# Two layers written out one after the other: the last output products moved behind the barrier into the next layer's block, weights loaded across it, the copy of x dropped

## The chip, the cores and the metric

The kernel runs on one core of one Trainium2 chip. The metric is the device time of one execution in microseconds (us), the median of several runs. The core has a matrix engine (TensorE, PE in the rows), a vector engine (VectorE, DVE), a scalar engine (ScalarE, ACT), GpSimd (POOL) and a sync engine (SyncE, SP) that issues DMA. Each engine works through its own list of instructions in order. They meet only at semaphores: an instruction can wait until a counter has reached a value, and raises a counter when it is done.

## The reference

The input x is 512 tokens of 2048 float32 features. Two layers are applied. `h` is the RMS norm of x; one projection makes everything else; four mixers (RWKV-7, mLSTM, latent attention, differential attention) produce 512 features each, gated by `silu(z)`:

```python
h = RMSNorm(x);  p = h @ W_in            # 2048 x about 7900
# p -> [ z | RWKV-7 group | mLSTM group | MLA group | differential-attention group ]
y = concat(beta_A*A, beta_B*B, beta_C*C, beta_D*D) * silu(z)
x = x + y @ W_out                        # 2048 x 2048
```

Layer 0 and layer 1 differ in one place of the RWKV-7 group. Layer 0 keeps its `v` as `v_first`. Layer 1 mixes it in:

```python
if v_res is None:
    v_first = v
else:
    v0, v_dn, v_up = v_res
    v = v + (v_first - v) * jax.nn.sigmoid(v0 + (v @ v_dn) @ v_up)
```

## The kernel before

All large products are made in three parts, since each float32 operand is split into a high and a low half (`w_hi`, `w_lo` for weights, `h_hi`, `h_lo` for activations). A weight step is one block of 128 rows by up to 512 columns. SP loads it into one of six `raw` buffers, the high half is made by ACT (`high_part`, L1234) in the first 32 steps and the last ones of a layer and by POOL (L746) in between, and POOL makes the low half (L756) into one of four split buffers. A step has four tiles (column blocks, or token blocks for the output), and a tile is three matmuls of 128x512. A layer has 256 steps of the projection (`project`, L785), and 64 of the output: 48 early ones (`out_early`), for the first twelve blocks of y, and 16 of the tail, for the last four (all `out_product`, L800). A group of 16 projection steps fills a PSUM bank per tile; ACT copies it out (`evacuate`, L1225) and stores it to DRAM, from where the mixers load it.

The mixers run in between on the same engines. Their small products depend on DVE and ACT, and PE fills the waits with projection tiles. The order is written out by hand: the table `FILL` says how many tiles PE takes at each named place of each head (`fill(name, h)`), and `planned` deals them out. Places named `to_...` take whatever is missing to the end of a group, so that a number changed ahead of one is paid back there. The last place is `rest`, which takes the remaining early output tiles.

The program starts with a block of its own. SP loads x (four tiles `x_tok`), parameters and constants, and copies x to the output in DRAM. ACT squares x (L424). Then comes a loop `nc.Fori(0, DEPTH)`, whose body is executed twice. In it: the mean of the squares (DVE L1601), its inverse root by `rstd` (ACT L1269, L1270, Ln and Exp, each with a table load), the diagonal (DVE L1614), a product with ones that spreads it (PE L837), a copy (ACT L1277), and the transposes of x (PE L834, L843) scaled by DVE (`scale_h`, L1621). Near the end of the layer x is loaded again from the output. `add_tile` (DVE L1893) adds finished output tiles to it. The tail, the last lines of the PE block, follows `rest`; `keep_x` on ACT stores x and squares it (L1547). Then all engines meet at a barrier that also clears the layer's semaphores (POOL L1953), and the loop jumps back.

Heads of RWKV-7 are taken in pairs `hp` of 0 to 3. PE waits there at L942 (for the gate of the pair before, DVE L1594), at L948 (for DVE L1709) and at L952 (for DVE L1740). `tanh_z` (ACT L1256) must run before the gate. At L917 the scores of the latent attention wait for DVE L1665, at L1156 those of the differential attention for ACT L1500.

In this kernel layer 0 mixes v as well, with a factor of zero (`half_flag`), since both layers are the same code.

Of the kernel before, what the change touches and what calls it, by code (L numbers as in the profile page):

```python
# [27 lines left out]
P = 128  # L28
# [45 lines left out]
TAIL = 4 * (len(OUT_PARTS) - 1)  # L74
EARLY = sum(q < TAIL for q, *_ in OUT)
# [4 lines left out]

Y_LOADS = STEPS - KT + 3 + N_RAW + N_SPLIT


def tiles_of(g):
    return 3 if g == G_MISC else 4


PROJ_TILES = [(n, m) for n in range(STEPS) for m in range(tiles_of(n // KT))]
# [10 lines left out]
    da_first=17, da_sums=(16, 10, 10, 10), da_scores=(8, 6, 6, 6), da_half=(13, 15, 18, 18), da_turned=(3, 3, 3, 3),  # L99
# [211 lines left out]
def build(nc, a, out):  # L311

    with ExitStack() as ctx:
# [81 lines left out]
        half_flag = small[:, 60:61]  # L395
        lam_init = small[:, 61:62]
        one_m_lam_init = small[:, 62:63]

        s_setup, s_setup_out, s_flags = sem("setup_loaded"), sem("x_kept"), sem("flags_set")
        s_setup_squared = sem("setup_squared")
        s_params_loaded = sem("params_loaded")
        s_setup_x = [sem(f"x_loaded_{i}") for i in range(NT)]
        neg_f32 = carve(D, P)

        with nc.Block() as block:
            @block.sync
            def _(sp):  # L410
                for i in range(NT):
                    sp.dma_start(x_tok[:, i, :], a["x"][0, i * P:(i + 1) * P, :]).then_inc(s_setup_x[i], 16)
                sp.dma_start(par_all[:], a["params"]).then_inc(s_params_loaded, 16)
                sp.dma_start(always[:], a["const"][:, 0:ALWAYS]).then_inc(s_setup, 16)
                sp.dma_start(neg_f32, a["const"][:, CONST["neg"][0]:CONST["neg"][0] + P]).then_inc(s_setup, 16)

                sp.dma_start(out[0], a["x"][0]).then_inc(s_setup_out, 16)

            @block.scalar
            def _(act):  # L420
                act.wait_ge(s_flags, 1)
                for i in range(NT):
                    act.wait_ge(s_setup_x[i], 16)
                    nc.scalar.activation(carve(0, D), x_tok[:, i, :], ACT.Square, accum_out=ms_parts[:, i, 0:1]  # L424
                                         ).then_inc(s_setup_squared, 1)
                    act.wait_ge(s_setup_squared, i + 1)

            @block.vector
            def _(dve):
                nc.vector.memset(small[:, 64:80], 0.0).then_inc(s_flags, 1)  # L430
                nc.vector.memset(v_first[:], 0.0).then_inc(s_flags, 1)
                nc.vector.memset(small[:, 0:60], 0.0).then_inc(s_flags, 1)
                nc.vector.memset(half_flag, 0.0).then_inc(s_flags, 1)
                nc.vector.memset(lam_init, 0.8 - 0.6).then_inc(s_flags, 1)
                nc.vector.memset(one_m_lam_init, 1.0 - (0.8 - 0.6)).then_inc(s_flags, 1)
                dve.wait_ge(s_setup, 32)
                nc.vector.tensor_copy(mask_ident, ident).then_inc(s_flags, 1)
                nc.vector.tensor_copy(neg, neg_f32).then_inc(s_flags, 1)
                dve.wait_ge(s_flags, 8)


# [81 lines left out]
        x_junk = da_pt[:, 0, :]  # L523
# [25 lines left out]

        s_lam_ready = sem("lam_ready")  # L550
        s_h_hi_ready = sem("h_hi_ready")
        s_par_ready = sem("par_ready")
        s_x_squares = sem("x_squares")
# [8 lines left out]
        s_hi_split = sem("hi_split")  # L562
        s_hi_by_act = sem("hi_by_act")
# [3 lines left out]
        s_raw_split = sem("raw_split")  # L567
        s_split_used = sem("split_used")
# [4 lines left out]
        s_out_kept = sem("out_kept")  # L573
# [115 lines left out]
        s_raw_loaded = [sem(f"raw_loaded_{s}") for s in range(N_RAW)]  # L689
# [12 lines left out]
        weight_steps = list(steps_of_weights())  # L702
# [7 lines left out]
        with nc.Fori(0, DEPTH) as layer:  # L710
            with nc.Block() as block:
                @block.sync
                def _(sp):

                    for n, (source, k, pieces) in enumerate(weight_steps):
                        part, early = divmod(n - Y_LOADS, 3)
                        if 0 <= part < 4 and early == 0:
                            ks = slice(3 * part, 3 * part + 3)
                            sp.wait_ge(s_split_used, STEPS - KT + 3 * part + 3)
# [6 lines left out]
                        if n >= N_RAW:  # L726
                            sp.wait_ge(s_raw_split, n - N_RAW + 1)
                        at = 0
                        for c0, width in pieces:
                            sp.dma_start(raw[:, n % N_RAW, at:at + width],  # L730
                                         a[source][layer, k * P:(k + 1) * P, c0:c0 + width]
                                         ).then_inc(s_raw_loaded[n % N_RAW], 16)
                            at += width

                @block.gpsimd
                def _(pool):

                    for n in range(len(weight_steps)):
                        pool.wait_ge(s_raw_loaded[n % N_RAW], raw_target[n])
                        if n >= N_SPLIT:  # L740
                            pool.wait_ge(s_split_used, n - N_SPLIT + 1)
# [18 lines left out]
                def _(pe):  # L760
# [52 lines left out]
                    def out_early(n, i):  # L813
                        q, c, k, first, _ = OUT[n - STEPS]
                        if i == 0:
                            pe.wait_ge(s_raw_split, n + 1)
                            if c == 0:
                                wait_y(k)
# [372 lines left out]
                    for n in range(STEPS + EARLY, ALL_STEPS):  # L1191
                        q, c, k, first, _ = OUT[n - STEPS]
                        if c == 0:
                            wait_y(k)
# [782 lines left out]
```

## Time and profile before

| | |
|---|---|
| median of 3 runs | 2497.51 us (2495.53 to 2502.27) |
| the profiled execution | 2498.22 us |
| its span, first to last instruction | 2496.5 us |
| mean granted TensorE clock | 0.982 of full speed |
| PE busy | 96% of the span |
| DVE, ACT, POOL busy | 47%, 25%, 69% |
| HBM traffic | 116 GB/s over the span |

A row of the timeline gives start, duration, engine, line, operation, operands and in brackets how long the engine was idle before it and what ended that wait. The projected end of a matmul is modelled, so that successive ones overlap in the rows.

### The profile page before, as it was taken

How to read it: one execution, taken by the hardware profiler on the slowest of the kernel's cores; microseconds unless marked ns; L12 is line 12 of the kernel's file. 1: busy time of each engine (PE TensorE's matmuls, PEld its weight loads, DVE VectorE, ACT ScalarE, POOL GpSimd, SP SyncE). 2: the span in 40 equal slices, each digit the busy share in tenths (PEclk: the TensorE clock that was granted, in tenths of full speed). 3: DMA queues.
4: the chain of work that ended last, by engine and by line, in shares of the span. 5: the costliest groups of instructions: out<-in, count | busy, mean ns of one | idle time of the engine just before them, and what ended most of it. 6: DMA issues, size and time to landing. Idle time of an engine off the chain costs nothing. (4 is left out here: it accounts for less than half of the span.)

```text
span 2496.5 us, 40525 instructions
## 1 busy us (share of the span) xinstructions
PE 2390.7 (96%) x16332; PEld 1798.2 (72%) x16332; DVE 1183.6 (47%) x1654; ACT 632.1 (25%) x1119; POOL 1724.5 (69%) x1228
## 2 busy tenths in 40 slices
PE   6999999999999999999979999999999999999998
PEld 4766677676777777777867677777777767777777
DVE  5122236656473774454260232376465637735442
ACT  4222212212121222333242223112121112223423
POOL 2675588567585877877636666877575767877875
PEclk9999999999999999999989999999999999999999
DMA  6622344223233435632336232532232234465323
GB/s 213 181 80 74 95 141 123 73 86 89 82 106 106 132 114 180 213 85 72 118 96 185 80 102 77 166 94 82 73 106 83 85 115 131 127 213 163 85 76 122
DMA packets 164293, 288.69 MB, mean 116 GB/s; under 512 B 29017, under 2 KB 36569, under 8 KB 162497
## 3 DMA queue, kind: packets, MB, share of 16 engines
q1 hardware_dynamic: 108864, 185.51, 26.5%
q10 hardware_dynamic: 55232, 100.51, 11.7%
q8 instruction: 130, 2.13, 0.4%
q14 instruction: 67, 0.54, 0.1%
HBM read 234.29 MB, written 55.84 MB: 116 GB/s over the span
## 5 line engine op out<-in xcount | busy, mean ns | idle before, releaser
L746 POOL TENSOR_SCALAR w_hi<-raw 128x512 fp32r<-128x512 f32 x552 | 897.2, 1625 | 547.7 <-PE ps_proj L785 481.5
L756 POOL TENSOR_TENSOR w_lo<-raw,w_hi 128x512 fp32r<-128x512 f32 (+1 forms) x640 | 831.9, 1301 | 174.0 <-ACT w_hi L1234 127.9
L785 PE MATMUL ps_proj<-h_hi,w_hi 128*128 128x512 f32 (+1 forms) x1760 | 735.6, 418 | 20.2 <-POOL w_lo L756 9.9
L785 PE MATMUL ps_proj<-h_lo,w_hi 128*128 128x512 f32 (+1 forms) x1760 | 691.6, 393 | 0.0
L785 PE MATMUL ps_proj<-h_hi,w_lo 128*128 128x512 f32 x1728 | 679.6, 393 | 0.0
L785 PEld LDWEIGHTS ps_proj<-h_hi,w_hi 128*128 128x128 f32 (+1 forms) x1760 | 332.0, 189 | 125.8 <-issue 38.2
L785 PEld LDWEIGHTS ps_proj<-h_lo,w_hi 128*128 128x128 f32 (+1 forms) x1760 | 332.6, 189 | 74.0 <-issue 11.6
L785 PEld LDWEIGHTS ps_proj<-h_hi,w_lo 128*128 128x128 f32 x1728 | 327.3, 189 | 71.8
L800 PE MATMUL ps_proj<-w_hi,h_hi 128*128 128x512 f32 x448 | 183.1, 409 | 3.9 <-DVE arena L1893 3.9
L800 PE MATMUL ps_proj<-w_hi,h_lo 128*128 128x512 f32 x448 | 175.3, 391 | 0.0
L800 PE MATMUL ps_proj<-w_lo,h_hi 128*128 128x512 f32 x448 | 174.7, 390 | 0.0
L1225 ACT ACTIVATE stage<-ps_proj 128x512 f32<-128x512 f32 (+1 forms) x118 | 70.5, 597 | 252.9 <-PE ps_proj L785 200.4
L785 PE MATMUL ps_proj<-w_hi,h_hi 128*128 128x512 f32 x256 | 107.6, 420 | 0.4 <-ACT stage L1225 0.4
L785 PE MATMUL ps_proj<-w_lo,h_hi 128*128 128x512 f32 x256 | 101.7, 397 | 0.0
L800 PEld LDWEIGHTS ps_proj<-w_hi,h_hi 128*128 128x128 f32 x448 | 84.3, 188 | 24.2 <-issue 8.1
L785 PE MATMUL ps_proj<-w_hi,h_lo 128*128 128x512 f32 x256 | 101.4, 396 | 0.0
L800 PEld LDWEIGHTS ps_proj<-w_lo,h_hi 128*128 128x128 f32 x448 | 84.4, 188 | 19.7 <-issue 3.4
L800 PEld LDWEIGHTS ps_proj<-w_hi,h_lo 128*128 128x128 f32 x448 | 84.2, 188 | 18.1
L1648 DVE TENSOR_REDUCE arena<-ps 128x1 f32<-128x128 f32 (+3 forms) x96 | 47.1, 490 | 97.7 <-PE ps L919 66.8
L1234 ACT ACTIVATE w_hi<-raw 128x512 fp32r<-128x512 f32 (+1 forms) x88 | 49.0, 561 | 168.0 <-PE ps_proj L785 78.0
L1269 ACT ACTIVATE arena<-ps 128x512 f32<-128x512 f32 x24 | 14.4, 598 | 276.9 <-PE ps L1141 137.5
L1529 ACT ACTIVATE arena<-ps,arena 128x128 f32<-128x128 f32 (+3 forms) x64 | 38.7, 615 | 134.7 <-DVE arena L1649 134.7
(354 smaller groups left out, 3202.6 us busy)
## 6 DMA issues: line engine op xcount, KB each, us to landing
raw<-in_w_in_dram SPq DMA_DIRECT2D x480, 256.0 KB, 2.7
raw<-in_w_out_dram SPq DMA_DIRECT2D x128, 256.0 KB, 3.1
projected<-stage ACTq DMA_DIRECT2D x116, 256.0 KB, 3.3
arena<-projected ACTq DMA_DIRECT2D x90, 256.0 KB, 3.1
arena<-out_dram ACTq DMA_DIRECT2D x2, 4096.0 KB, 17.6
gated_hi<-arena ACTq DMA_DIRECT2D x24, 256.0 KB, 2.5
gated_lo<-arena ACTq DMA_DIRECT2D x24, 256.0 KB, 2.9
h_hi<-gated_hi SPq DMA_DIRECT2D x8, 768.0 KB, 6.0
```

The lines of the kernel that those rows point to most:

```text
L746: nc.gpsimd.tensor_scalar(hi, src, 1.0, None, ALU.mult).then_inc(s_hi_split, 1)
L756: nc.gpsimd.tensor_tensor(lo, src, hi.bitcast(F32), ALU.subtract).then_inc(s_raw_split, 1)
L785: last = mm(ps_proj[rows, m, :], lhsT, rhs, start=(k == 0 and j == 0), stop=(k == KT - 1 and j == len(products) - 1))
L800: last = mm(bank[:, i, :], lhsT, rhs, start=(first and j == 0), stop=(last_k and j == 2))
L1225: nc.scalar.activation(stage[0:rows, m, :], ps_proj[0:rows, m, :], ACT.Copy).then_inc(s_proj_copied, 1)
L1234: nc.scalar.activation(w_hi[:, n % N_SPLIT, 0:widths[n]], raw[:, n % N_RAW, 0:widths[n]], ACT.Copy).then_inc(s_hi_by_act, 1)
L1269: link(nc.scalar.activation(dst, src, ACT.Ln, scale=1.0 / n, bias=eps))
L1529: nc.scalar.activation(da_p[:, b, 0:(i + 1) * P], ps[:, b, 0:(i + 1) * P], ACT.Exp, scale=da_rq[:, 4 * half + b:4 * half + b + 1], bias=da ...
L1648: link(v.tensor_reduce(mx[:, b:b + 1], ps[:, b, 0:(i + 1) * P], AX, MAX))
```

## The change

The loop becomes a Python loop over `DEPTH + 1` sections. A section has a *tail* (the last 16 output steps of the layer before it) if it isn't the first, and a *body* (the layer's own work) if it isn't the last. The barrier stands after each body, so ahead of the tail. The counters of the weight pipeline are no longer cleared and count through; SP loads ten steps beyond the body's early products, across the barrier, and POOL splits four.

```diff
+LOADED_AHEAD = STEPS + EARLY + N_RAW + N_SPLIT
+ROWS_OF_MEAN = (slice(0, 3), slice(3, 4))
 FILL = dict(
-    begin=4, la_first=36, la_sums=18, la_v=4, la_heads=(7, 7, 7, 7), la_qk=(12, 11, 12, 11),
+    begin=4, la_first=36, la_sums=18, la_v=4, la_heads=(7, 7, 7, 7), la_qk=(15, 11, 12, 11),
-    rw_first=8, rw_lora=(10, 9, 9, 9), rw_factors=(31, 36, 36, 32), rw_turned=(4, 4, 4, 4), rw_v=(2, 2, 2, 2),
+    rw_first=8, rw_lora=(10, 13, 9, 9), rw_factors=(31, 32, 32, 34), rw_turned=(4, 4, 4, 4), rw_v=(2, 2, 2, 2),
-    da_first=17, da_sums=(16, 10, 10, 10), da_scores=(8, 6, 6, 6), da_half=(13, 15, 18, 18), da_turned=(3, 3, 3, 3),
+    da_first=21, da_sums=(16, 10, 10, 10), da_scores=(8, 6, 6, 6), da_half=(13, 15, 18, 15), da_turned=(3, 3, 3, 3),
...
-        with nc.Fori(0, DEPTH) as layer:
+        for layer in range(DEPTH + 1):
+            tail, body = layer > 0, layer < DEPTH
+            base, tail_base = layer * ALL_STEPS, (layer - 1) * ALL_STEPS
+            loaded_to = min(base + LOADED_AHEAD, DEPTH * ALL_STEPS)
+            split_to = min(base + HI_LAST, DEPTH * ALL_STEPS)
+            mixes_v = layer > 0
...
-                sp.dma_start(out[0], a["x"][0]).then_inc(s_setup_out, 16)
...
+                    if tail:
+                        for c in range(4):
+                            n0 = STEPS + EARLY + c * TAIL_K
+                            if c < 3:
+                                order = [(n, i) for n in range(n0, n0 + TAIL_K) for i in range(NT)]
+                            else:
+                                order = [(n, i) for i in range(NT) for n in range(n0, n0 + TAIL_K)]
...
+                    if tail:
+                        pe.wait_ge(s_out_added, 12)
...
-                    pe.wait_ge(s_rs_diag, 1)
-                    mm(ps_proj[:, 0, :], ones, rs_diag, start=True, stop=True).then_inc(s_rs_mm, 1)
+                    for n, tiles in enumerate(ROWS_OF_MEAN):
+                        pe.wait_ge(s_rs_diag, n + 1)
+                        mm(ps_proj[:, n, tiles.start * P:tiles.stop * P], ones, rs_diag[:, tiles, :],
+                           start=True, stop=True).then_inc(s_rs_mm, 1)
...
+                    if mixes_v:
+                        pe.wait_ge(s_rw_v_shifted, 1)
+                        for j in range(4):
+                            last = mm(ps[64:96, 0, :], rw_vdn[:, j, :], rw_v[:, j, 1:T + 1], start=(j == 0), stop=(j == 3))
...
-                    rstd(rs_x, ms, D, EPS).then_inc(s_x_mean, 1)
+                    def root_of_mean(n, tiles):
+                        act.wait_ge(s_x_squares, n + 1)
+                        nc.scalar.activation(rs_x[:, tiles], ms[:, tiles], ACT.Sqrt, scale=1.0 / D, bias=EPS).then_inc(s_x_mean, 1)
...
+                    for n, tiles in enumerate(ROWS_OF_MEAN):
+                        if tail and n:
+                            for m in range(N_SPLIT):
+                                high_part(base + m)
...
+                        tanh_z(4 + hp, rw_z, rw_e)
                         fill("rw_gate", hp)
-                        tanh_z(4 + hp, rw_z, rw_e)
...
-                    act.wait_ge(s_setup_out, 16)
-                    act.dma_start(x_tok, x_dram).then_inc(s_x_prefetched, 16)
+                    act.dma_start(x_tok, x_dram if tail else a["x"][0].rearrange("(i p) d -> p i d", p=P)
+                                  ).then_inc(s_x_prefetched, 16)
...
-            nc.all_engine_barrier(sems_to_clear=of_layer)
+            if layer < DEPTH:
+                nc.all_engine_barrier(sems_to_clear=of_layer)
```

Also in the change: in the first section SP issues the first weights right behind x in the same block, and ACT loads constants and parameters on its own queue. x is squared there in two halves per tile. Layer 0 no longer runs the v mixing (four products `rw_vdn`, four `rw_vup`, the third tanh, three vector operations per pair), layer 1 no longer copies into `v_first`. The transposes wait only for the first three column blocks of x, the inverse root is made for token tiles 0 to 2 and then for tile 3.

What the instruction order shows. The first place is PE at the end of a layer. Before, the list runs through from the early tiles (into `ps_proj`) to the tail and the loop's branch; these are its last rows:

```order
L800 MATMUL ps_proj<-w_hi,h_hi 128x512 [waits raw_split]
L800 MATMUL ps_proj<-w_lo,h_hi 128x512
L800 MATMUL ps_proj<-w_hi,h_lo 128x512
...
L711 UNCONDITIONAL_BRANCH
L710 REGISTER_ALU [waits barrier_Pool_Activation_PE_DVE_SP_release]
L710 COMPARE_AND_BRANCH
```

In the change (L779 is the output product) the barrier and two branches stand between the last early tile and the tail's first tile, which goes to `ps`:

```order
L779 MATMUL ps_proj<-w_hi,h_hi 128x512
L779 MATMUL ps_proj<-w_lo,h_hi 128x512
L779 MATMUL ps_proj<-w_hi,h_lo 128x512
L684 UNCONDITIONAL_BRANCH
L738 UNCONDITIONAL_BRANCH [waits barrier_Pool_Activation_PE_DVE_SP_release]
L779 MATMUL ps<-w_hi,h_hi 128x512 [waits raw_split]
L779 MATMUL ps<-w_lo,h_hi 128x512
```

So PE now stops between early tiles and tail, in both layers. POOL arrives at the same barrier only behind its last two steps, each a high and a low half; L1999 is the clearing of semaphores:

```order
L725 TENSOR_SCALAR w_hi<-raw 128x512 [waits split_used,raw_loaded_0]
L735 TENSOR_TENSOR w_lo<-raw,w_hi 128x512 [waits hi_split]
L725 TENSOR_SCALAR w_hi<-raw 128x512 [waits split_used,raw_loaded_1]
L735 TENSOR_TENSOR w_lo<-raw,w_hi 128x512 [waits hi_split]
L684 UNCONDITIONAL_BRANCH
L1999 ISA [waits barrier_Pool_Activation_PE_DVE_SP_gather]
L713 UNCONDITIONAL_BRANCH
```

The third place is ACT at the gate of RWKV pair 1. Before, the tanh of z (L1256) stands behind the four bank copies of a projection group:

```order
L1270 ACTIVATE arena<-arena 128x512 [waits act_order]
L1225 ACTIVATE stage<-ps_proj 128x512 [waits stored_0,proj_done]
L1228 DMA projected<-stage 128x512 [waits proj_copied]
...
L1225 ACTIVATE stage<-ps_proj 128x512 [waits stored_3,split_used]
L1228 DMA projected<-stage 128x512 [waits proj_copied]
L1256 ACTIVATE arena<-arena 128x512 [waits y_kept,z_loaded]
L1436 ACTIVATE arena<-arena 4x512 [waits ml_gate_abs]
L1437 ACT_TABLE_LOAD
```

Now it stands ahead of them (as L1245), while the mLSTM gate's steps (now L1488) stay behind:

```order
L1259 ACTIVATE arena<-arena 128x512 [waits act_order]
L1245 ACTIVATE arena<-arena 128x512 [waits y_kept,z_loaded]
L1213 ACTIVATE stage<-ps_proj 128x512 [waits stored_0,proj_done]
L1216 DMA projected<-stage 128x512 [waits proj_copied]
...
L1213 ACTIVATE stage<-ps_proj 128x512 [waits stored_3,split_used]
L1216 DMA projected<-stage 128x512 [waits proj_copied]
L1488 ACTIVATE arena<-arena 4x512 [waits ml_gate_abs]
L1489 ACT_TABLE_LOAD
```

## Rows read from the trace of the kernel before

**Rows 1.** The page, part 1: busy us, share of the span, instructions.
```profile
PE 2390.7 (96%) x16332; PEld 1798.2 (72%) x16332; DVE 1183.6 (47%) x1654; ACT 632.1 (25%) x1119; POOL 1724.5 (69%) x1228
```

**Rows 2.** Waits of PE, whole run: waiting line, releaser, total us, times, longest us.
```profile
PE ps L942 <- DVE arena L1594: 8.9, 2, 4.4
PE ps_proj L785 <- ACT stage L1225: 7.8, 4, 4.0
PE ps L948 <- DVE arena L1709: 5.7, 2, 2.9
PE ps L1156 <- ACT arena L1500: 4.0, 2, 2.7
PE ps_proj L800 <- DVE arena L1893: 3.9, 2, 2.0
...
PE ps L917 <- DVE arena L1665: 3.6, 2, 1.8
...
PE ps L952 <- DVE arena L1740: 2.6, 2, 1.3
...
PE ps L942 <- DVE arena L1700: 1.6, 2, 0.8
```

**Rows 3.** Busy time in eleven stretches of low clock inside the layers: first, and sum.
```profile
190.00:200.20 10.20, 10.20 (x18) 4.01 (x18) 1.78 (x4) 0.00 (x0) 0.00 (x0) 0.50 0.10 27
...
sum 57.90, PE 53.73 PEld 33.09 DVE 26.97 ACT 24.29 POOL 7.61; mean PE 4.88 PEld 3.01 DVE 2.45 ACT 2.21 POOL 0.69
```

**Rows 4.** Timeline of the start: start us, duration, engine, operation.
```profile
13.19 1.91 ACT L424 ACTIVATE arena<-arena 128x2048 f32<-128x2048 f32 x1
...
20.84 0.60 ACT L1277 ACTIVATE arena<-ps_proj 128x512 f32<-128x512 f32 x1 [2.08 <-PE ps_proj L837]
...
27.80 0.63 ACT L1234 ACTIVATE w_hi<-raw 128x512 fp32r<-128x512 f32 x1 [4.92 <-DMA raw<-in_w_in_dram]
...
29.90 0.79 PE L785 MATMUL ps_proj<-h_hi,w_hi 128*128 128x512 f32 x1 [6.74 <-POOL w_lo L756]
```

**Rows 5.** Chain of the work that ended last: the second layer's tail begins.
```profile
2446.44 10.88 PE ps L800 x48
```

**Rows 6.** Timeline of POOL at the end of the second layer's early products.
```profile
2448.18 1.49 POOL L746 TENSOR_SCALAR w_hi<-raw 128x512 fp32r<-128x512 f32 x1
2449.76 2.54 POOL L756 TENSOR_TENSOR w_lo<-raw,w_hi 128x512 fp32r<-128x512 f32 x2
```

**Rows 7.** Timeline between the layers.
```profile
1250.12 0.39 PE L800 MATMUL ps_proj<-w_hi,h_lo 128*128 128x512 f32 x1
1260.94 3.68 PE L834 MATMUL ps<-always,arena 128*128 128x128 f32 x16 [10.43 <-issue]
...
1265.90 0.60 ACT L1277 ACTIVATE arena<-ps_proj 128x512 f32<-128x512 f32 x1 [2.56 <-PE ps_proj L837]
...
1269.94 0.80 PE L785 MATMUL ps_proj<-h_hi,w_hi 128*128 128x512 f32 x1 [1.89 <-POOL w_lo L756]
```

**Rows 8.** Timeline at the end of the run.
```profile
2489.57 0.39 PE L800 MATMUL ps_proj<-w_hi,h_lo 128*128 128x512 f32 x1
...
2492.18 0.34 ACTq L1566 DMA_DIRECT2D out_dram<-arena  x1
```

**Rows 9.** DMA issues in the last 11 us: KB each, median us to landing.
```profile
out_dram<-arena ACTq DMA_DIRECT2D x4, 256.0 KB, 2.4
```

**Rows 10.** Timeline around RWKV pair 2 of the second layer.
```profile
1826.74 0.63 ACT L1256 ACTIVATE arena<-arena 128x512 f32<-128x512 f32 x1 [0.46 <-ACT stage L1225]
...
1836.70 0.69 DVE L1709 TENSOR_TENSOR arena<-arena 128x512 f32<-128x512 f32 x1
...
1839.57 1.02 PE L948 MATMUL ps<-arena,always 128*128 128x512 f32 x2
...
1860.69 0.69 DVE L1740 TENSOR_TENSOR arena<-arena 128x512 f32<-128x512 f32 x1
...
1864.94 0.27 PE L952 MATMUL ps<-always,arena 128*128 128x128 f32 x1
```

More of the change, by code:

```diff
@@ L393, in build @@
         lam_prod = small[:, 29:31]
[L395 to L405, printed above, removed]
-        neg_f32 = carve(D, P)
[L408 to L415, printed above, removed]
-                sp.dma_start(out[0], a["x"][0]).then_inc(s_setup_out, 16)
[L419 to L439, printed above, removed]
+        sqrt_set = small[:, 60:61]
+        neg_f32 = carve(D, P)
         rg = Region()
@@ new lines, in _ @@
+                    if body:
+                        act.wait_ge(s_setup, 32)
+                        link(nc.scalar.activation(sqrt_set, eps_col, ACT.Sqrt))
+                    if tail:
+                        for n in range(HI_LAST, ALL_STEPS):
+                            high_part(tail_base + n)
+                            q, c, _, _, last_k = OUT[n - STEPS]
+                            if last_k and c:
+                                keep_x(c - 1)
+                                if body:
+                                    for i in range(NT):
+                                        square_x(i, c - 1, G)
@@ new lines, in _ @@
+                    if not body:
+                        for i in range(NT):
+                            keep_x(3, slice(i, i + 1))
+                        act.wait_ge(s_out_kept, 16 * (4 * (DEPTH - 1) + 7))
+                        return
+                    for n, tiles in enumerate(ROWS_OF_MEAN):
+                        if tail and n:
+                            for m in range(N_SPLIT):
+                                high_part(base + m)
+                        for i in range(tiles.start, tiles.stop):
+                            if tail:
+                                act.wait_ge(s_out_added, 12 + i + 1)
+                                square_x(i, 3, G)
+                            else:
+                                act.wait_ge(s_x_loaded[i], 16)
+                                for half in range(2):
+                                    square_x(i, half, D // 2)
+                        root_of_mean(n, tiles)
@@ L1307, in _ @@
                     fill("la_sums")
+                    if tail:
+                        act.wait_ge(s_out_kept, 16 * 4 * layer)
                     for i in range(NT):
@@ new lines, in _ @@
+                    if tail:
+                        for c in range(3):
+                            for i in range(NT):
+                                add_tile(TAIL + c, i, (ps, ps_proj)[c % 2])
+                    for n, tiles in enumerate(ROWS_OF_MEAN):
+                        if tail:
+                            for i in range(tiles.start, tiles.stop):
+                                add_tile(TAIL + 3, i, ps_proj)
+                        if body:
+                            inverse_root(n, tiles)
```

272 lines of the change are left out of this document (147 added, 125 removed).

## The prediction

> **What bounds the kernel now.** I began with the page: TensorE is busy 96% of 2496.5 us [rows 1]. Nothing else comes near, so the time is PE's work, plus 106 us in which it does nothing, plus what it loses when its clock falls. Next I read its waits [rows 2]: eight kinds inside the layers hold 38.1 us, each with one place per layer. Then the granted clock in narrow windows [rows 3]: eleven stretches inside the layers run at 0.50, 1.2 instead of 2.4 GHz. PE is busy for 53.7 us in them, so about 26.9 us are lost. Last the timelines of the three places outside the layers: the start, where the first projection product stands at 29.90 [rows 4], the gap between the layers, from 1250.51 (1250.12 + 0.39) to 1269.94, 19.4 us [rows 7], and the end, from 2489.96 to 2496.5, 6.5 us [rows 8].
>
> The unit of the sum is a tile of three matmuls. 48 matmuls take 10.88 us [rows 5], so 0.227 us each and 0.68 us per tile.
>
> **The start, 6.5 us less.** Today x is squared until 15.1, the mean is spread and copied at 20.84, and then ACT waits 4.92 us for the first weights, which land at 27.8 behind the copy of x [rows 4]. That copy is dropped and the weights are issued right behind x. The squares' last operation began at 13.19, so the last x tile had landed by then. I put its landing at 14.4, with constants now sharing the DMA. Two half squares (2.4 us by the 1.91 of a whole one and a second fixed part) end at 16.8. Sum, root, reciprocal, diagonal and spreading for one tile take some 1.5 us, without the two table loads, so the copy stands at 18.3. From the copy to the first product it took 4.04 us between the layers [rows 7]. First product at 22.4, 7.5 us earlier; I take off 1.0 for more matmuls at low clock there. If the weights were late again, the gain would be 2; nothing lies below that but a landing after 27.8.
>
> **Between the layers, 11.7 us less.** The 19.4 us hold waiting for stores, the barrier, the jump, transposes, mean and two table loads. Now PE ends the tail at a time E and goes on with 16 transposes, 3.7 us [rows 7]. Beside them DVE adds the last tile, ACT makes four high halves and squares that tile, and its root and diagonal follow, in about the same time. The copy can't stand before E+3.7, the transposes' end; today it stands 4.96 us behind the first transpose, table loads included. I take E+4.5. From there it is 4.04 us today, less POOL's low half of 1.27 [rows 6], which is done earlier now: 2.8. That is 7.3 us of gap. The tail's last column block in the new order wants its fourth weight step some 0.4 us early. 19.4 - 7.3 - 0.4 = 11.7. The four high halves and their low halves are hidden behind the transposes; without that cover they cost up to 4 us.
>
> **The end, 2.6 us less.** Today four stores are issued with squares in between, the last at 2492.18, landing 2.4 us later [rows 8, 9], and barrier and clearing take the remaining 1.9. Without squares the last store goes out 0.9 us after the last product, and lands by +3.3; with 0.6 for the closing branch this is 3.9 instead of 6.5.
>
> **Two barriers inside, 17.0 us more.** This is the new wait. PE stops after the last early tile at 2446.44 [rows 5]. POOL is then in the middle of its queue: a high half at 2448.18, and a low half that ends at 2449.76 + 1.27 = 2451.03 [rows 6], 4.6 us after PE. POOL can't be quicker, since the buffer of its last step is only freed by PE's last early step. Barrier and clearing: the run's end gives 1.9, from the landing at 2492.18 + 2.4 [rows 8, 9] to 2496.5. The gap between the layers gives 5.8: by the same distances its last store landed at 1250.51 + 2.22 + 2.4 = 1255.1, and PE starts at 1260.94 [rows 7], the jump back included. There is no jump back now, so I take 1.9 + 0.3 and keep 5.8 for the range. After 6.8 us of idleness the clock will be low for a while. A low stretch is 57.9 / 11 = 5.3 us on average and would cost 2.6; part of it falls into the pause itself, so I take 1.7 (0 to 5.1). 8.5 us per layer, twice. Everything queued behind it (tail, next layer) moves by it. Nobody else gains from the pause, as the tail's first four steps are split already.
>
> The Trainium skill, page "Runtime: NRT & Kernel Launch", section "Instruction fetch mechanics", says that a taken branch to a target outside the prefetched pages waits for a DMA fetch. By that rule the loop's jump would explain the longer 5.8; but if the branches at each section's end leave the prefetched part too, each barrier costs 5.8 and the sum loses 7.2.
>
> **Inside the layers, 28.5 us less.** By the rows of waits [rows 2]: L917, 3.6 us: three tiles more ahead (2.04 per layer, needed 1.8), all gone. L948, 5.7: four tiles more at pair 1 (2.72 against 2.87), 5.4 gone. L952, 2.6: two tiles more at pair 3, gone. L1156, 4.0: `da_first` and the place before it get five more, 3.4 against 2.7, gone. L942 behind L1700, 1.6: the v mixing leaves the first layer, 0.8 gone. L785 behind the bank copy, 7.8: two tiles moved behind it, 1.36 per layer, 2.7 gone; the stores that ACT waits for stay. L800 behind L1893, 3.9: the three tiles that waited move behind the transposes, but the half probabilities are ready only 0.8 us earlier, 1.6 gone.
>
> L942 behind L1594, 8.9, is the largest, and here I look at what is late next. The tanh at 1826.74 [rows 10] can run before the bank copies, so the gate is early enough. But ACT's mLSTM gate step stays behind the copies and is only the tanh's 0.63 us and a short queue earlier, and DVE takes it before L1709. So L1709 ends at 1837.39 - 1.5 = 1835.9, while PE would now reach L948 at 1839.57 - 4.45 = 1835.1. At L952 PE would come at 1835.9 + 25.4 - 2.7 (four tiles less) = 1858.6, with L1740 done at 1861.38 - 1.5 = 1859.9. Of 4.45 us 2.3 remain in layer 1; in layer 0, where DVE has three operations less (at least 0.69 each), 3.7. Together 6.0. A giver that keeps its slack is the same place taken alone: today PE comes to L952 3.5 us after DVE and gives 2.7.
>
> 3.6 + 5.4 + 2.6 + 4.0 + 0.8 + 2.7 + 1.6 + 6.0 = 26.7, plus eight products dropped in layer 0, 1.8: 28.5.
>
> **The clock, 11 us less.** The eleven low stretches follow the waits above, mostly within a few us. If all fell away, 26.9 us would return; if they only wander, none. Of the waits' 38.1 us 26.7 go, but the sparse stretches of small matmuls stay, such as the longest (18 matmuls in 10.2 us [rows 3]). I take 40%.
>
> **Sum.** 6.5 + 11.7 + 2.6 - 17.0 + 28.5 + 11 = 43.3. Against the profiled execution's 2498.2 that is 2454.9. The median of the runs is 0.7 lower, less than I can resolve: 2455.
>
> **The rivals.**
> *The waits move.* A tile given to one wait is taken from another place. If half of the 26.7 us reappear at the givers, and the clock gives nothing, the gain is 19: 2479. For it: pair 2 above. Against it: the slack of 3.5 us there, which the four tiles alone don't use up. 0.17.
> *The clock comes back whole.* 16 us more than in the sum, 2439. For it: low stretches stand right behind waits; against it: the longest has only a short one. 0.13.
> *The barriers cost a fetch.* 5.8 instead of 2.2, and the clock low twice as long: 10.6 less gain, 2465. This is also what the skill's rule gives when it applies to each section. 0.12.
> *Slower: the clock falls more often.* PE now stops longer inside the tail, and every pair has a sparse stretch like the one at 190. A fall of 10.2 us costs 5.1. With (43.3 + 7.5) / 5.1, ten more such falls would eat the gain and make it slower: 2506. Eight pairs and two tails could give ten. Against it: those stretches exist now and ran at full clock but for a few. 0.05.
> *The change doesn't do what it says.* The start could still wait for weights and the boundary for something else; without both 2473, inside the range. It is in the forecast's share.
>
> **How the numbers follow.** The forecast has 0.53. A measurement of this kernel can tell 0.3%, 7.5 us, from no change. The forecast and the first three rivals are faster, 0.95, of which I give 0.02 to no change, since all doubts on one side together (clock 11, waits 13, barriers 10.6) reach 2489, and 0.02 more to slower: faster 0.91, same 0.03, slower 0.06. The range reaches from the whole clock, 2437, to just beyond the moved waits, 2482.
>
> **What would show it.** First projection product near 22; about 7 us of PE idleness between early tiles and tail, twice, ended by POOL's last low half; some 7 us between the tail's end and the first product; last product to end 4 us; waits at L917, L948 of pair 1 and L1156 gone, new ones of about 1 us at pair 2. I am wrong if PE's waits inside the layers still add up to over 25 us, if the two pauses exceed 10 us each, or if the low clock inside the layers isn't less than before.

## The result, and the profile after

The changed kernel takes 2478.85 us (median; 2472.99 to 2480.24), the kernel before 2499.4 in the same series (2495.53 to 2502.27): a ratio of 0.9914, 95% interval 0.9892 to 0.9937. It is faster by 20 us, where I had forecast 43, and the interval excludes no change. The profiled execution took 2478.23 us with a span of 2476.4. This is part 1 of its page, beside [rows 1]:

```profile
PE 2380.3 (96%) x16320; PEld 1793.5 (72%) x16320; DVE 1181.2 (48%) x1633; ACT 616.1 (25%) x1092; POOL 1726.7 (70%) x1228
```

The waits of PE over the whole run (waiting line, releaser, total us, times, longest us), beside [rows 2]:

```profile
PE ps_proj L764 <- ACT stage L1213: 16.9, 5, 8.0
PE ps L779 <- PEq L1999: 14.2, 2, 7.3
PE ps L947 <- DVE arena L1769: 11.6, 5, 5.3
PE ps L830 <- DMA arena<-in_const_dram: 9.1, 1, 9.1
PE ps L830 <- DMA arena<-in_x_dram: 4.0, 2, 2.0
PE ps L875 <- DVE arena L1980: 3.8, 4, 1.3
```

The rows that the prediction wanted to see go have gone: the gate (L942), L917, L1156 and L952 are missing. But two others grew. The wait for ACT's bank copy (L785 behind L1225 before, 7.8 us) is 16.9, and that for the squared key (L948 behind L1709 before, 5.7) is 11.6. In two of its five places the bank copy takes 8.05 and 6.61 us, and the squared key twice 5.3, at another pair than before. Added up over all rows of this view, with PE's stretch from the first projection product to the last early tile of each layer, the waits inside the layers are 26.2 + 27.2 = 53.4 us before and 24.0 + 25.0 = 49.0 after.

The granted clock in narrow windows is the other half. The view has us, busy time of PE, PEld, DVE, ACT and POOL, clock, DMA share and GB/s; these are the low stretches inside the layers, beside [rows 3]:

```profile
577.90:584.70 6.80, 4.05 (x8) 2.59 (x9) 6.55 (x9) 1.68 (x3) 0.90 (x1) 0.51 0.14 39
...
960.00:966.80 6.80, 4.07 (x10) 3.21 (x11) 0.00 (x0) 3.10 (x4) 2.18 (x2) 0.50 0.75 258
1806.50:1813.30 6.80, 4.13 (x8) 2.62 (x9) 6.56 (x9) 1.76 (x3) 0.81 (x1) 0.50 0.16 41
...
2188.80:2199.00 10.20, 5.75 (x14) 4.50 (x15) 0.00 (x0) 3.10 (x4) 2.92 (x3) 0.50 0.92 314
sum 40.80, PE 28.20 PEld 20.95 DVE 22.08 ACT 11.02 POOL 7.11; mean PE 4.03 PEld 2.99 DVE 3.15 ACT 1.57 POOL 1.02
```

Seven stretches instead of eleven, with 28.2 us of PE's work in them instead of 53.73. The clock differs between executions of one kernel more than the waits do: in a second profiled execution of the changed kernel, below, there are six such stretches with 25.2 us. The four shown are the four places of the new long waits: each wait ends inside a stretch at 1.2 GHz or just ahead of one.

Where the 20.1 us between the two spans lie (the first column is read from PE's timeline: its first projection product, last early tile, first tail product, next first projection product):

| stretch | before | after | gain | forecast |
|---|---|---|---|---|
| start to first projection product | 29.90 | 24.43 | 5.5 | 6.5 |
| inside layer 0 | 1176.9 | 1163.3 | 13.7 | |
| inside layer 1 | 1176.5 | 1171.0 | 5.5 | 39.5 for both |
| pauses at the two barriers | 0 | 14.2 | -14.2 | -13.6 |
| tail and gap between the layers | 63.1 | 53.4 | 9.7 | 11.7 less 1.7 of clock |
| last tail to the end | 50.1 | 50.1 | 0 | 2.6 less 1.7 of clock |

So the outside went nearly as forecast, and 20 of the 23 missing us are missing inside the layers. The experiments ask why.

### The profile page after: what moved, and what is told of

It is laid out like the page before. It is cut to its first block and busy times, and to the rows that moved or that the text cites. A ratio compares the mean times of both kernels' runs of the same rounds, so it can differ in the third digit from the quotient of the medians.

```text
span 2476.4 us, 38951 instructions
## 1 busy us (share of the span) xinstructions
PE 2380.3 (96%) x16320; PEld 1793.5 (72%) x16320; DVE 1181.2 (48%) x1633; ACT 616.1 (25%) x1092; POOL 1726.7 (70%) x1228
## 5 line engine op out<-in xcount | busy, mean ns | idle before, releaser
L779 PE MATMUL ps_proj<-w_hi,h_hi 128*128 128x512 f32 x448 | 183.1, 409 | 0.4 <-POOL w_lo L735 0.4
L779 PE MATMUL ps_proj<-w_hi,h_lo 128*128 128x512 f32 x448 | 174.9, 390 | 0.0
L779 PE MATMUL ps_proj<-w_lo,h_hi 128*128 128x512 f32 x448 | 174.5, 390 | 0.0
L764 PE MATMUL ps_proj<-w_hi,h_hi 128*128 128x512 f32 x256 | 109.2, 426 | 14.7 <-ACT stage L1213 14.7
L779 PEld LDWEIGHTS ps_proj<-w_hi,h_hi 128*128 128x128 f32 x448 | 84.2, 188 | 21.3 <-issue 4.0
L779 PEld LDWEIGHTS ps_proj<-w_lo,h_hi 128*128 128x128 f32 x448 | 84.2, 188 | 19.6 <-issue 3.4
L779 PEld LDWEIGHTS ps_proj<-w_hi,h_lo 128*128 128x128 f32 x448 | 84.1, 188 | 18.0
L1258 ACT ACTIVATE arena<-ps 128x512 f32<-128x512 f32 x24 | 14.4, 599 | 275.4 <-PE ps L1140 143.5
L764 PEld LDWEIGHTS ps_proj<-w_hi,h_hi 128*128 128x128 f32 x256 | 49.9, 195 | 30.1 <-ACT stage L1213 15.5
```

The source lines that it names most:

```text
L764: last = mm(ps_proj[rows, m, :], lhsT, rhs, start=(k == 0 and j == 0), stop=(k == KT - 1 and j == len(products) - 1))
L779: last = mm(bank[:, i, :], lhsT, rhs, start=(first and j == 0), stop=(last_k and j == 2))
L1258: link(nc.scalar.activation(dst, src, ACT.Ln, scale=1.0 / n, bias=eps))
```

## The experiments

All ratios are against the kernel before on the same chip, with 95% intervals; waits come from each kernel's own profile.

### The changed kernel once more

> The changed kernel itself, as the measure for the three edits that share its chip. Expected: 2479 us (2473 to 2484), some 19 us below the kernel before, PE waiting again 8.0 us for a bank copy in one layer and 6.6 in the other, 5.3 us twice for the squared key of RWKV pair 2, and 6.9 and 7.3 us at the two barriers. If those waits were chance of one execution, they would differ here.

Measured: 2477.94 us, ratio 0.9916 (0.9895 to 0.9937). Its waits are 17.1 us for the bank copy, 11.1 for the squared key, 14.3 at the barriers. The waits belong to the program, not to one execution. The low clock does so only in part: windows set in the same way give 25.16 us of PE's work at about half clock inside the layers, against 28.20 above.

### The bank copy ahead of the queue again

```diff
-ml_gate=(12, 12, 12, 12)
+ml_gate=(12, 12, 12, 13)
```

ACT's timeline of the changed kernel shows why I suspected that place. The first three banks of group z_da are copied, then come the two stores of `keep_y`, a wait until they have landed and four loads, and only then the fourth copy, for which PE waits (the value in brackets is idle time ahead, and what ended it):

```profile
952.75 0.60 ACT L1213 ACTIVATE stage<-ps_proj 128x512 f32<-128x512 f32 x1 [0.46 <-ACT stage L1213]
953.38 0.33 ACTq L1216 DMA_DIRECT2D projected<-stage  x1
953.80 0.39 ACTq L1253 DMA_DIRECT2D gated_hi<-arena  x1
954.22 0.80 ACTq L1254 DMA_DIRECT2D gated_lo<-arena  x1
960.20 0.33 ACTq L1545 DMA_DIRECT2D arena<-projected  x1
...
961.52 0.46 ACTq L1561 DMA_DIRECT2D arena<-in_x_dram  x1
962.08 0.60 ACT L1213 ACTIVATE stage<-ps_proj 128x512 f32<-128x512 f32 x1 [8.72 <-issue]
```

And PE:

```profile
962.73 0.79 PE L764 MATMUL ps_proj<-w_hi,h_hi 128*128 128x512 f32 x1 [8.05 <-ACT stage L1213]
```

Before, the fourth copy of this group stood right behind the third:

```profile
976.20 0.60 ACT L1225 ACTIVATE stage<-ps_proj 128x512 f32<-128x512 f32 x1 [0.46 <-ACT stage L1225]
...
977.91 0.60 ACT L1225 ACTIVATE stage<-ps_proj 128x512 f32<-128x512 f32 x1 [1.11 <-issue]
```

The table's places are filled from one list in order. The new numbers hand out two tiles fewer by the end of the last mLSTM gate than the old ones did, so the last tile of z_da falls out of `ml_gate` into `to_z_da`, a place that ACT reaches only after waiting for its stores of y and issuing the next loads.

> One tile more in the last mLSTM gate place (13 for 12), so that the place before the last differential stage has no product of PE left and ACT makes the four bank copies of group z_da ahead of keep_y and its DMA issues again. Theory (the copy stands behind the waits and DMA issues that follow that place): PE's waits for ACT's bank copy fall from 16.9 us to about 2.3, the one of 8.05 and the one of 6.61 are gone, and nothing else appears: 2479 - 14.6 = 2464 us, 2459 if the low clock behind these waits goes too. Rival (the wait only stands in for one that comes next: PE then arrives 7 us earlier at the first differential product, where the kernel before waited 2.7 us for ACT's square): PE waits there for 3 us or more, and the time stays above 2472.

Measured: 2463.84 us, ratio 0.9857 (0.983 to 0.9884). The bank copy holds PE for this:

```profile
PE ps_proj L764 <- ACT stage L1213: 2.5, 2, 1.3
```

14.1 us less than the changed kernel, as the first theory said. PE did not wait for ACT's square at the next place instead, but for 2.2 us for a constant (L1155). So some 14.6 us of waits went, 2.2 came, and the gain is no larger than the wait itself. One number in the table is worth three quarters of what the change gained inside the layers.

### DVE's mLSTM gate steps, behind the squared key

```diff
                         v.tensor_tensor(rw_sq, rw_kk, rw_kk, MUL).then_inc(s_rw_kk_sq, 1)
+                        if hp == 2:
+                            dve.wait_ge(s_ml_gate_log, 1)
+                            link(v.scalar_tensor_tensor(out=ml_sg[forget, :], in0=ml_gt[forget, :], scalar=0.0, in1=ml_sg[forget, :], op0=MIN, op1=SUB))
+                            v.tensor_tensor_scan(ml_gt[forget, :], carry[forget, :], ml_sg[forget, :], 0.0, MUL, ADD).then_inc(s_ml_gates, 1)
```

The same lines under `hp == 1`, behind the gate of pair 1 (L1884 to L1887), are taken out.

The second grown wait, in DVE's timeline of the changed kernel:

```profile
1796.08 1.64 DVE L1626 TENSOR_TENSOR arena<-arena 128x512 fp32r<-128x512 f32 x1
1800.51 1.05 DVE L1886 SCALAR_TENSOR_TENSOR arena<-arena 4x512 f32<-4x512 f32 x1 [2.79 <-ACT arena L1489]
1801.60 1.21 DVE L1887 TENSOR_TENSOR_SCAN arena<-always,arena 4x512 f32<-4x512 f32 x1
1802.84 1.61 DVE L1766 TENSOR_TENSOR arena<-arena 128x512 f32<-128x512 f32 x1
...
1806.23 1.64 DVE L1767 SCALAR_TENSOR_TENSOR arena<-arena,par 128x512 f32<-128x512 f32 x1
1807.90 0.49 DVE L1768 TENSOR_SCALAR arena<-arena,par 128x512 f32<-128x512 f32 x1
1808.42 0.69 DVE L1769 TENSOR_TENSOR arena<-arena 128x512 f32<-128x512 f32 x1
```

PE leaves the gate of pair 1 at once (1796.34), passes its filling tiles and stands:

```profile
1809.17 2.08 PE L947 MATMUL ps<-arena,always 128*128 128x512 f32 x2 [5.35 <-DVE arena L1769]
```

DVE loses 2.79 us until ACT has made the logarithm behind its bank copies, and 2.3 us for the two steps themselves.

> DVE's two mLSTM gate steps (0.7 + 1.6 us, and 2.8 us of waiting for ACT's logarithm ahead of them) stand behind the squared key of RWKV pair 2 instead of ahead of it. Theory (PE's wait of 5.3 us at pair 2, in both layers, is DVE held by the gate's logarithm and scan): the wait falls from 5.3 to under 0.5 us, twice, 2479 - 10 = 2469 us, two or three less if the low clock follows. Rival (DVE is late by the length of its other operations, which take 1.6 us each beside POOL, or by the tail of pair 1): the wait stays above 3 us, 2475 or more. Second rival: it reappears at the next wait of the pair, for the factors, and the time does not move.

Measured: 2476.57 us, ratio 0.9909 (0.9888 to 0.993): no gain that can be told from none. The second rival was right, as PE's waits show (L951 is the factors):

```profile
PE ps L951 <- DVE arena L1806: 7.4, 3, 4.2
...
PE ps L947 <- DVE arena L1769: 2.0, 4, 0.8
```

### The same steps in DVE's idle time

The two steps now stand in pair 2 just ahead of `dve.wait_ge(s_rw_rstd, hp + 1)`, where DVE waits 4.1 us for ACT in any case.

> DVE's two mLSTM gate steps stand in pair 2's own idle time, 3.8 us in which DVE waits for ACT's inverse root, instead of ahead of pair 2's squared key. Behind that key, in the run before, PE's wait of 5.4 us fell to 0.8 but came back as up to 4.2 us at the factors, since DVE did the same work between the two. Theory (DVE is the bound of pair 2 from the gate to the factors, so only work taken out of that stretch counts): the wait at the squared key stays near 0.8 us and the one at the factors falls by the 2.3 us of the two steps, to 0.2 to 2 us per layer; PE's waits at both places together fall from 12.0 to about 4.8 us in the run, 2478 - 7 = 2471 us. Rival (ACT's tanh, its table loads and the squared key's root set the factors, not DVE's own work): the sum stays at 9 us or more and the time at 2475 or more.

Measured: 2467.09 us, ratio 0.9869 (0.9849 to 0.9888), 11 us less than the changed kernel:

```profile
PE ps L947 <- DVE arena L1769: 2.8, 7, 0.8
...
PE ps L951 <- DVE arena L1802: 1.9, 2, 1.0
```

The waits are as the theory said, 4.7 us in sum instead of the 12.0 of the second execution above; they gave 7.3 us. The rest fits the clock: the low stretches behind this wait (577.90 and 1806.50 above) are gone, and PE's work at about half clock inside the layers is 18.9 us instead of 25.2 to 28.2, worth 3.1 to 4.6 us.

### The tanh back, without and with that edit

```diff
-                        tanh_z(4 + hp, rw_z, rw_e)
                         fill("rw_gate", hp)
+                        tanh_z(4 + hp, rw_z, rw_e)
```

> The changed kernel with the tanh of z behind the bank copies again, as in the kernel before. It tests the largest term of the prediction, 6.0 us for the gate of RWKV pair 1. Theory (with the mLSTM gate steps on DVE behind that gate, an earlier gate frees no PE time: the wait is only taken at pair 2's squared key instead): PE waits 4.5 us per layer for the gate again, the 5.3 us at the squared key fall to some 1 us, and the time stays within 3 us of 2478. Rival (the term as predicted, since both waits stand side by side): 6 us or more slower, 2484 or above.

> The same with the mLSTM gate steps in DVE's idle time of pair 2. With them out of the way, the place of the tanh should count: against the 2467 us of that edit with the tanh ahead, PE waits 4.5 us for the gate in each layer and less than 1 us at the squared key, so 2467 + 8 = 2475 us (2471 to 2478). Rival (the gain of that edit was the clock's, and the tanh counts for nothing here either): within 2 us of 2467.

Measured: the first 2475.57 us, ratio 0.992 (0.99 to 0.994), the second 2479.59 us, ratio 0.9936 (0.9916 to 0.9955). These two ran beside a kernel before of 2493.93, so their ratios are what to compare: 0.992 against 0.9916 for the changed kernel, and 0.9936 against 0.9869 with the steps in idle time. So in the changed kernel no worth of the early tanh can be seen; the two intervals together leave room for 7 us either way. PE's waits are the sharper measure. In the first of the two PE waits at the gate again, and not at the squared key:

```profile
PE ps L940 <- DVE arena L1621: 8.9, 2, 4.5
...
PE ps L947 <- DVE arena L1769: 0.8, 3, 0.4
```

With up to 0.3 us at the factors that is 10.0 us with the late tanh, against 11.8 and 12.0 at the same three places in the two executions with the early one: the early tanh saves PE no waiting at all.

Why the earlier gate brings the squared key no sooner is seen in DVE's chain from the gate's two steps to the squared key. Here, where PE stood at the gate, POOL had stood behind PE for 7.78 us, and the chain takes 6.5 us, from 1798.71 to 1805.20:

```profile
1798.71 0.68 DVE L1886 SCALAR_TENSOR_TENSOR arena<-arena 4x512 f32<-4x512 f32 x1
...
1803.93 1.60 POOL L725 TENSOR_SCALAR w_hi<-raw 128x512 fp32r<-128x512 f32 x1 [7.78 <-PE ps_proj L764]
1804.22 0.98 DVE L1769 TENSOR_TENSOR arena<-arena 128x512 f32<-128x512 f32 x1
```

In the changed kernel PE goes on, so POOL goes on making halves, and the same chain takes 8.6 us, from 1800.51 to 1809.11.

With DVE's steps out of the way the tanh is worth 0.67%, 17 us, twice what I expected; by the medians alone, from two chips, it is 12.5 us. PE's waits explain some 6 of them (8.9 at the gate come, 1.9 at the squared key and 0.9 at the factors go). Much of the rest fits the clock: by the same windows PE works 18.9 us at half clock inside the layers with the early tanh and 32.9 with the late one, 7 us of difference. That adds up to 13; the remaining few us I can't assign, and the intervals leave room for them. With the late tanh, on the other hand, DVE's steps in idle time gain nothing: on one chip 2479.59 us against 2475.57, 4 us longer, for which I have no account.

### POOL's queue two steps shorter at the barrier

```diff
-HI_FIRST, HI_LAST = 2 * KT, STEPS + EARLY + 4
+HI_FIRST, HI_LAST = 2 * KT, STEPS + EARLY + 2
-LOADED_AHEAD = STEPS + EARLY + N_RAW + N_SPLIT
+LOADED_AHEAD = HI_LAST + N_RAW
```

> POOL's queue ends two steps earlier ahead of each barrier, and SP loads two steps fewer across it; their high halves are made by ACT and the low ones by POOL behind the barrier. Theory (the pause at the barrier is POOL's two last steps of 2.8 us each beyond PE's end, plus 1.9 us of barrier and clearing and some 0.3): POOL is done 5.7 us earlier, just ahead of PE, the pause falls from 6.9 and 7.3 to about 2.3 us, 2479 - 9.5 = 2470 us, and the low clock of the tail's first products is gone or shorter: up to 5 less. Rival (the steps that are split only behind the barrier are late, since the raw loads of two steps start late too): PE waits in the tail's third and fourth step for what the pause gave back, 2476 to 2480.

Measured: 2463.8 us, ratio 0.9856 (0.983 to 0.9882), 14.1 us less. In the changed kernel POOL's last low half and PE's restart are

```profile
1191.44 1.26 POOL L735 TENSOR_TENSOR w_lo<-raw,w_hi 128x512 fp32r<-128x512 f32 x1
...
1194.63 0.76 PE L779 MATMUL ps<-w_hi,h_hi 128*128 128x512 f32 x1 [6.94 <-PEq L1999]
```

and with this edit

```profile
1185.50 1.30 POOL L735 TENSOR_TENSOR w_lo<-raw,w_hi 128x512 fp32r<-128x512 f32 x1
...
1189.58 0.47 PE L779 MATMUL ps<-w_hi,h_hi 128*128 128x512 f32 x1 [2.19 <-PEq L1999]
```

POOL is done at 1186.8, ahead of PE, and the pause is the bare barrier: 2.19 us. Both pauses sum to 4.4 instead of 14.2, and no wait takes their place in the tail. The other 4 us are the clock: behind each of the two pauses of the changed kernel PE's first ten or eleven matmuls are some 0.43 us apart instead of 0.23, 2 us each time, and here none is. In the first 3.4 us of the tail the changed kernel does 8 matmuls, this one 15:

```profile
1194.60:1198.00 3.40, 3.37 (x8) 2.72 (x9) 1.64 (x10) 1.48 (x2) 0.00 (x0) 0.50 0.11 38
```

```profile
1189.50:1192.90 3.40, 3.32 (x15) 2.76 (x16) 1.64 (x10) 2.86 (x5) 1.02 (x1) 1.00 0.02 5
```

### The structure alone, and the table alone

> The changed kernel with the table of filling tiles and the place of the tanh of the kernel before: both layers written out, tail beside the next layer's first work, no v mixing in the first layer, and nothing moved inside the layers. Read from the two traces: start 5.5 less, gap and low clock between the layers 9.7 less, two barriers 14.2 more, end 0, v mixing some 3 less: 2499.5 - 4 = 2495.5 us (2490 to 2499). Rival (the gain inside the layers came from the structure, by the v mixing and by another phase of the clock, not from the table): 2485 or less.

> The kernel before with nothing changed but the table of filling tiles and the place of the tanh. Layer 1, where the structure changes nothing inside, gained 5.5 us from the table between the two traces, so twice that is expected here: 2499.5 - 11 = 2488.5 us (2484 to 2493), with the new bank-copy waits of 8 and 6.6 us and those of some 5 us at pair 2 seen in this kernel as well. If those waits came from the new layer boundary instead, they are missing here and the kernel gains 25 or more: 2474.

Measured: structure alone 2493.93 us, ratio 0.9978 (0.9966 to 0.9991); table and tanh alone 2492.91 us, ratio 0.9976 (0.9965 to 0.9987). Each is worth 5 to 6 us, 11 in sum, and together they give 20. The table alone is worth about half of the 11 us expected of it. The table alone brings both new waits into the kernel before:

```profile
PE ps_proj L785 <- ACT stage L1225: 17.9, 3, 8.2
...
PE ps L948 <- DVE arena L1709: 11.1, 4, 5.4
...
PE ps L952 <- DVE arena L1740: 4.3, 2, 2.2
```

so they come from the table, not from the new boundary. By the sum over all rows of the view the waits inside the layers are even longer with the table alone, 28.3 + 29.1 = 57.4 us against 53.4 before. A part of what the two give only together is the clock: its low stretches over the whole run, read in steps of 1.7 us and counted under 0.75, add up to 88 us before, 78 with the structure, 82 with the table, and with both to 66 and 55 in two executions. Why they add up so stays open. For the factors (L952) a part is seen in pair 1 of the second layer, which mixes v in both kernels: PE waits 2.10 us there with the table alone and 0.16 in the changed kernel. DVE's chain from the squared key to the last factor takes 25.2 us and 23.9, and the kernel before copies into `v_first` in it, which the changed one no longer does in this layer:

```profile
1728.87 0.72 DVE L1721 COPY v_first<-arena 128x512 f32<-128x512 f32 x1
```

### The three edits together

The bank copy's tile, the two POOL steps and the gate's steps in idle time, in one kernel.

> The changed kernel with three edits: one tile more in the last mLSTM gate place, two high halves less ahead of each barrier, the gate's two steps in DVE's idle time. The first two gave 14.1 us each alone, and they lie in different stages, so both add up unless the clock's low stretches were the same: 2478 - 28 = 2450 us, and 7 less if the third gives what is expected of it: 2443 us (2439 to 2449). Rival (part of each gain was the same clock coming back, or the waits move again): 2455 or more.

Measured: 2437.74 us (2436.36 to 2438.86), ratio 0.9755 (0.9739 to 0.9771), 2.4% faster than the kernel before, 40 us faster than the changed one and just below the range expected. The three gains (14.1, 14.1 and 10.9 by medians) add up. Inside the layers PE's waits are 13.7 + 16.1 = 29.8 us, and four low stretches are left there, 3.4 us each:

```profile
787.10:790.50 3.40, 3.40 (x10) 2.62 (x9) 3.22 (x6) 0.00 (x0) 0.00 (x0) 0.50 0.25 74
963.90:967.30 3.40, 3.40 (x12) 2.22 (x11) 0.00 (x0) 2.74 (x4) 1.14 (x1) 0.60 1.02 424
1949.90:1953.30 3.40, 3.40 (x23) 2.62 (x16) 2.91 (x6) 1.95 (x3) 0.00 (x0) 0.67 0.02 5
2000.90:2004.30 3.40, 3.40 (x8) 2.04 (x8) 3.26 (x5) 0.00 (x0) 0.63 (x1) 0.69 0.29 77
sum 13.60, PE 13.60 PEld 9.50 DVE 9.39 ACT 4.68 POOL 1.77; mean PE 3.40 PEld 2.38 DVE 2.35 ACT 1.17 POOL 0.44
```

The wait for the squared key is 3.6 us here. The 2.2 us for a constant (L1155) that came with the bank copy's tile are in it again; the factors (L951) wait 2.0 us instead of 0.2, and nothing else over 1 us is new.

## Why the prediction was wrong

**The start** (6.5, measured 5.5). The loading of the weights no longer decides, as forecast. But the first product was forecast at 22.4 and stands at 24.43, 2.0 us late; of the 1.0 us taken off for the low clock only some 0.3 was needed, as eight matmuls instead of six are 0.42 us apart or more there. The mean's last copy stands at 20.71 instead of 18.3. The last tile of x had landed by 14.26, near my 14.4, but ACT starts squaring at 9.29 and makes eight halves, most of them 1.18 us apart, so the last ends at 19.0 and not at 16.8. Behind the copy the first product follows after 3.7 us, near the 4.04 taken from the other boundary. The last thing that it waits for is POOL's low half, made behind ACT's high half, which ACT makes only at 22.34:

```profile
17.98 1.06 ACT L1271 ACTIVATE arena<-arena 128x1024 f32<-128x1024 f32 x1
24.43 0.79 PE L764 MATMUL ps_proj<-h_hi,w_hi 128*128 128x512 f32 x1 [1.42 <-POOL w_lo L735]
```

**Between the layers** (gap 7.3). PE's transposes start at 1240.78, its first projection product stands at 1248.00: 7.2 us. Right.

**The end** (3.9 us behind the last product). It is 2476.4 - 2472.83 = 3.6. Right. The gain of 3.0 went into the tail ahead of it, 2.3 into the half clock behind the second barrier and 0.5 into a late low half.

**The barriers** (6.8 us of pause each, 1.7 of clock). 6.94 and 7.28 us, and low stretches of 6.8 us behind each, partly inside the pause, which cost about 2 us each. POOL's last low half ends at 1192.70 and PE starts 1.93 us later, so the 1.9 was right and the 5.8 of the rival "a fetch" was not: the bare barrier takes 2.19 us with its branches. The rule of the Trainium skill, page "Runtime: NRT & Kernel Launch", section "Instruction fetch mechanics", on taken branches does not show here. This term was right in size, but I took the pause as given, although its cause stood in the same paragraph: two steps too many in POOL's queue.

**Inside the layers, waits** (28.5). This step failed. The total of PE's waits there fell by 4.4 us, and eight dropped products gave an estimated 1.8. It failed in two terms.

"L785 behind the bank copy, 2.7 gone." On the old places this held and more: of 7.8 us, 16.9 - 8.05 - 6.61 = 2.2 are left. But 14.7 us appeared at one more place of each layer. I had counted the tiles that the table adds in front of each wait, and `to_z_da`'s extra tile among them as cover. I did not ask whether that tile is the last of its group, and what stands ahead of its copy in ACT's queue. So in all this wait grew by 9.1 us, where 2.7 were forecast as gone. Restoring the tile gave 14.1 us.

"L942 behind L1594, 6.0." I had seen that DVE's steps stay behind ACT's copies and that pair 2 would be late next, and priced what is left at 2.1 us in layer 1 and 0.7 in layer 0. It was 5.3 in both. Two sizes were off, and in layer 1 they account for it. PE arrives 2.4 us earlier than I took it to: from the gate to the squared key it took 9.92 us before, a part of it at half clock behind the wait, and 7.48 now that the wait is gone. I had shifted the old stretch as it stood. And DVE arrives 2.0 us later. It starts the gate's two steps 1.5 us earlier, as I had said, but its chain from there to the squared key takes 8.6 us instead of 6.6. POOL stood for 7.51 us there before, while PE waited, and now works beside it. The 0.8 that I had left at the squared key, 2.4 and 2.0 make 5.2 of the 5.35 us measured. With the early tanh undone PE waited no longer than with it and no difference in time can be seen, so the term is about zero, not 6.0; with DVE's steps elsewhere it is worth more than I had hoped.

Beside these two terms, waits outside the eight kinds that I had priced grew by 4.2 us, from 15.3 to 19.5. The largest are L875 behind L1980 (3.8 us, 1.2 before), L1140 (2.0) and L1130 (1.0), neither of which waited before; the run with the table alone has them too.

**The clock** (11). PE's work at half clock inside the layers fell from 53.73 to 28.20 us, which by the prediction's own measure returns 12.8 us, and 14.3 by the second execution. The size was about right, though part of it is the luck of where waits fall: I took 40% of the low clock as gone with 26.7 us of waits, and about half went with 4.4. 4.4 + 1.8 + 12.8 = 19.0, and the two rows inside the layers gained 13.7 + 5.5 = 19.2.

The rival "the waits move" named the time that was measured, 2479 us, but by luck: it gave the clock nothing. Its picture, half of the waits coming back at the givers, fits the 4.2 us of small waits and not the rest: one tile crossed a border between two places, and one chain on DVE became due. The mark by which I would be wrong, over 25 us of waits inside the layers, was met with 49.0. By this count it was set too low, since 53.4 less the 26.7 of the forecast is 26.7, over 25 as well; of the eight kinds that the forecast priced 29.5 us are left, where it said 11.4. The stated chances don't add up either: by the sentence that gives them, no change has 0.02 and slower 0.07, not 0.03 and 0.06. With both causes taken out the sum comes near the forecast, 2478 - 14.1 - 10.9 = 2453 beside 2455. That is a sum of single runs, and it owes a part of its closeness to the clock.

## What to carry to other kernels

When a table of filling work is retuned, follow the running sum of tiles to every border where a group ends, and read what the engine that empties the bank has in its queue there; one tile on the wrong side cost 14 us. A wait that ends in a serial chain is paid at the chain's next reader: take work out of the chain up to the last one, and start the chain earlier too, since neither half gave anything alone here. A wait that is removed also sets the helpers going beside each other, so a chain timed while they stood is too short. Ahead of a barrier stop each helper's queue where the main engine stops; work queued ahead for later is paid there.

## What the runs showed of the hardware

A long wait can cost more than its length here. After a pause of 6.9 us the granted clock of the tail's first 3.4 us was 0.50, after one of 2.19 us it was 1.00, and taking 9.9 us of pauses out gave 14.1. For the bank copy it was not so: 14.6 us of waits gone, 2.2 come, and 14.1 gained. In the kernel with three edits the low stretches of the whole run are 28 us, against 88 before.

DVE's operations with two inputs from the arena last 0.69 us, 0.98 or some 1.65 for one shape. In the row list above L1766 takes 1.61 and L1767 1.64 while POOL is making low halves; behind 1807.3, where POOL has stopped, L1769 takes 0.69. Not every one beside POOL is longer: the second L1766, left out there, takes 0.69 at 1805.50, between two of POOL's operations. POOL's rows:

```profile
1801.98 1.92 POOL L735 TENSOR_TENSOR w_lo<-raw,w_hi 128x512 fp32r<-128x512 f32 x1
...
1805.88 1.43 POOL L735 TENSOR_TENSOR w_lo<-raw,w_hi 128x512 fp32r<-128x512 f32 x1
```

POOL's own halves are longer too, 1.92 and 1.43 instead of 1.28. That agrees with the Trainium skill, page "SBUF — State Buffer", section "SBUF: two separate sides", which says that the two engines take turns on a shared pair of ports for a whole operation. The chain above, 6.5 us while POOL stood and 8.6 beside it, shows what it costs. So a chain on DVE has to be priced by what POOL does beside it. No run took POOL's work away and left PE's waits as they were.
